# Fourteen input projections as three products of rounded parts, with GpSimd making the weights' low parts and the keys ahead of the low-rank products

## The chip, the cores and the metric

The kernel runs on one core of one Trainium2 chip. The metric is the device time of one execution in microseconds (us). The core has five engines, each with its own queue of instructions in program order: TensorE (matrix products into PSUM), VectorE, ScalarE, GpSimd and SyncE (which only issues transfers). They wait for each other by semaphores.

## What is computed

One layer of a streaming encoder for 512 tokens of width 1024, in float32. The tokens are normalized and modulated to h; h is multiplied by one combined input matrix whose columns feed three groups of heads; their outputs go through an output projection; a top-4-of-32 mixture of experts follows.

```python
cond = silu(c); mod = cond @ ada_w + ada_b          # 6 x 1024: sh1, sc1, g1, sh2, sc2, g2
h  = rms_norm(x, norm1) * (1 + sc1) + sh1
zp = h @ w_in                                       # columns: RWKV 1024, pool 256, q 512, k 512, v 512, f 8
# RWKV group: z = z + (previous token's z - z) * mu, then r, k, v and the inputs of three low-rank products
w_log = -softplus(-(w0 + tanh(wd) @ w_up)) - 0.5;  a = sigmoid(a0 + ad @ a_up);  g = sigmoid(gd) @ g_up
kk = k * k_k; kk = kk / norm(kk); k = k * (1 + (a - 1) * k_a)      # then a recurrence over the tokens
# pool group: trailing means of z over 2, 4, 8, 16 tokens, minus z, a small matrix per group
# fox group: softmax(q k^T / 8 + D[t] - D[s]) v with D = cumsum(log_sigmoid(f + b))
x = x + g1 * (concat(y_rwkv, y_pool, y_fox) @ w_out)
h = rms_norm(x, norm2) * (1 + sc2) + sh2;  x = x + g2 * moe(h);  out = rms_norm(x, norm_f)
```

## The kernel before

The input projections are worked feature by feature. hT holds h transposed as eight blocks of 128 features by 512 tokens. A **set** is one block of 128 output columns: eight products (k = 0..7) of a 128x128 block of weights with hT[k] (128x512), added up in one PSUM bank. There are 23 sets: eight "rw" (the RWKV columns), four "q", four "k", two "pz" (pool), one "f" of 8 columns, and four "v", where tokens and features change places. A float32 product appears in the trace as two matmul records, so a set has 16. The experts' weights, in contrast, are split already: ScalarE rounds them to float32r (w_hi, L1490), VectorE subtracts (w_lo, L1496), and TensorE makes three products of rounded parts for each (L2147).

The order of the work is written out once, in `plan()`, and every engine walks the same list `STEPS` and does its own part of each step. A **job** is a step with a PSUM bank; three banks are used in turn, so TensorE starts job n only when job n-3 has been read (`read_by`). Who reads a job stands in `READERS`: ScalarE copies rw, q, k, v and pz; VectorE reads "ada" and "rk"; "f" is read first by VectorE (L1033), then by ScalarE.

In a step "rw", ScalarE copies the bank to one of two buffers, and VectorE shifts it by one token and mixes (L968, L969, semaphore `shifted`); ScalarE's copy of rw n waits for the shift of rw n-2. Behind each rw, q and k step stands a step "acc": VectorE adds one of sixteen 1 MB pieces of `ada_w`, scaled by a value of cond, to a running sum of 128x2048 (L957, or L959 for the first of eight). The sum of eight pieces is then multiplied by a row of ones in four "ada" jobs (L1220), behind the first q set for the first half, between the value sets for the second.

SyncE's queue (`late_load`) brings these pieces into three buffers: piece i waits for sum i-2. The input weights arrive in six blocks of 512 columns in two buffers, block n waiting for the last job of block n-2. All are in one queue in order: blocks rw 0-3 and rw 4-7, pieces 0 to 4, two loads of `ada_b`, the q block, pieces 5 to 8, the k block, pieces 9 to 12, the pool and f block, pieces 13 to 15, the v block.

Before the list, ScalarE and VectorE each scale four blocks of hT (L723, L889), and VectorE builds masks and other constants (L893 to L920). GpSimd builds masks at the start, then waits for rw 7, fills 128x1024 with zeros and writes them to 17 blocks of `y_rows` (8.7 MB, L636), then makes the window sums of the pool columns (L643 to L648) and small products in the solve stage (L658 to L665).

"lora" are six low-rank products, "kkn" two sums for the norm of kk. At step kkn VectorE runs a chain (L980 to L1002); at pz 0 ScalarE takes exponentials (L767 to L771) and VectorE makes elementwise products (L1007 to L1019) that the solve stage needs. At step f VectorE reads the bank, waits for ScalarE's logarithm, scans (L1062) and finishes the pool windows (L1077 to L1082); only behind that does it read the "ada" jobs between the values. The fox attention, the solve stage, the recurrence, the output projection and the experts follow.

Of the kernel before, what the change touches and what calls it, by code (L numbers as in the profile page):

```python
# [15 lines left out]
F32 = mybir.dt.float32  # L16
# [62 lines left out]
def plan():  # L79

    def acc(i):
        return [("acc", i)]

    def turned(first):
        return [("ada", b) for b in range(first, first + 4)]

    steps = []
    for n in range(8):
        steps += [("rw", n)] + acc(n)
    steps += [("q", 0)] + turned(ADA_FIRST)  # L90
    for n in range(4):
        steps += ([("q", n)] if n else []) + acc(8 + n)
    steps += [("lora", n) for n in range(6)]
    steps += [("kkn", ct) for ct in range(CT)]
    for n in range(4):
        steps += [("k", n)] + acc(12 + n)
    steps += [("rk", ct) for ct in range(CT)]
    steps += [("pz", 0), ("pz", 1), ("f", 0)]
    for t in range(TT):
        steps += [("v", t), ("ada", ADA_FIRST + 4 + t)]  # L100
    pairs = FH * TT // 2
    early = 2
    steps += [("fox", u) for u in range(early)]
    steps += [("trAV", t) for t in range(TT)] + [("pm", 0)] + [("trBK", t) for t in range(TT)] + [("pm", 1)]
    solve = []
    for q in range(2):
        for kind in ("MP", "M"):
            solve += [(kind, q, par) for par in range(2)]
    fill = [[("NP", 0, 0), ("NP", 0, 1)], [("NP", 1, 0), ("NP", 1, 1)], [("NV", 0), ("NV", 1)]]
    for lv in range(1, LEVELS):  # L110
        solve += [("T", q, lv) for q in range(2)]
        if lv <= len(fill):
            solve += fill[lv - 1]
        for q in range(2):
            if lv < LEVELS - 1:
                solve.append(("XA", q, lv))
            solve.append(("XB", q, lv))
    solve += [("W", t) for t in range(TT)]
    for kind in ("QY", "GH"):
        solve += [(kind, q, cc) for q in range(2) for cc in range(2)]  # L120


    done = early
    for n, s in enumerate(solve):
        steps.append(s)
        while (done - early) * len(solve) < (n + 1) * (pairs + 2 - early):
            steps.append(("fox", done))
            done += 1
    while done < pairs + 2:
        steps.append(("fox", done))  # L130
        done += 1
    return steps
# [3 lines left out]
JOBS = [s for s in STEPS if s[0] not in ("fox", "acc")]  # L136
JOB = {s: n for n, s in enumerate(JOBS)}


# [5 lines left out]
def build(nc, a, out):  # L145
    with ExitStack() as ctx:
# [78 lines left out]
        R0 = early.enter_context(nc.sbuf_tensor("R0", [P, LATE], F32))  # L225
        Wt = early.enter_context(nc.sbuf_tensor("Wt", [P, 24576], F32))
        W3 = lambda off, x, y: Wt[:, off:off + x * y].rearrange("p (x y) -> p x y", x=x)
        R3 = lambda off, x, y: Rc(off, off + x * y).rearrange("p (x y) -> p x y", x=x)

        blk = [W3(4096 * s, KT, 512) for s in range(2)]  # L230

        def pair(off):
# [111 lines left out]
        h_act = sem("h_act")  # L344
        h_dve = sem("h_dve")
        bias2_in = sem("bias2_in")
        late_in = [sem(f"late_in{s}") for s in range(3)]
# [4 lines left out]
        cst_pool = sem("cst_pool")  # L352
        cst_dve = sem("cst_dve")
        cond_sig = sem("cond_sig")
# [75 lines left out]
        bias_lo = sem("bias_lo")  # L430
        bias_raw = sem("bias_raw")
        gm_rdy = sem("gm_rdy")
# [73 lines left out]
        def _(sp):  # L506
# [36 lines left out]
            def w_out_part(lo, hi, landed):  # L543
                sp.dma_start(w_out_sb[:, lo:hi, :], w_out_v[:, lo:hi, :]).then_inc(landed, 16)

            w_out_part(5, KT, wout_in)
            sp.dma_start(x_sb, a["x"][0].rearrange("(t p) d -> p t d", p=P)).then_inc(x_in, 16)
# [16 lines left out]
        def blk_ready(eng, b):  # L564
            n = BLK_OF[b]
            count = 16 * (n // 2 + 1)
            pf = BLK_OF[("pf", 0)]
            if n % 2 == pf % 2 and n >= pf:
                count += 16
            eng.wait_ge(blk_in[n % 2], count)  # L570


        @block.gpsimd
        def _(pool):
# [57 lines left out]

            job_done(pool, ("rw", 7))
            zero_src = Wt[:, 11264:11264 + D]
            link(g.memset(zero_src, 0.0))
# [37 lines left out]
        def _(act):  # L673
# [48 lines left out]
            for k in range(1, KT, 2):  # L722
                s.activation(hT[:, k, :], hT[:, k, :], ACT.Identity, scale=modc[:, KT + k:KT + k + 1],  # L723
                             bias=modc[:, k:k + 1]).then_inc(h_act, 1)

            for step in STEPS:
                kind = step[0]
# [29 lines left out]
                if kind == "rw" and step[1] >= 2:  # L757
                    act.wait_ge(shifted, step[1] - 1)
                if kind == "q" and step[1] == 2:
                    for ct in range(CT):  # L760
                        act.wait_ge(kk_raw, ct + 1)
                        s.activation(Kh[:, ct, :], Bh[:, ct, :], ACT.Square).then_inc(kk_sq, 1)
                if kind == "pz" and step[1] == 0:
                    for ct in range(CT):
# [52 lines left out]
                elif kind == "W":  # L817
                    ins = s.activation(W12[step[1]], b.rearrange("p (h w k) -> p h w k", h=RH, w=2), ACT.Copy)
                elif kind == "QY":
                    q, cc = step[1], step[2]  # L820
                    ins = s.activation(of_chunks(Yin, q, cc), b.rearrange("p (c j w s) -> p c j w s", c=CT, j=2, w=2)[:, :, :, 1, :],
                                       ACT.Copy)
                elif kind == "GH":
                    q, cc = step[1], step[2]
                    act.wait_ge(y_zero, 16)
                    ins = s.activation(GH[:, :, 4 * q + cc:4 * q + cc + 3:2, :],
                                       b.rearrange("p (j x m) -> p x j m", j=2, x=CT), ACT.Copy)
                ins.then_inc(act_read, 1)
                if kind == "f":
                    act.wait_ge(act_read, reads_through("A", step))  # L830
# [16 lines left out]
        def _(dve):  # L847
# [40 lines left out]
            for k in range(0, KT, 2):  # L888
                v.tensor_scalar(hT[:, k, :], hT[:, k, :], modc[:, KT + k:KT + k + 1], modc[:, k:k + 1],  # L889
                                ALU.mult, ALU.add).then_inc(h_dve, 1)  # L890

            dve.wait_ge(cst_pool, 1)
# [26 lines left out]
            link(v.reciprocal(rcnt[:], rcnt[:]))  # L919
            v.memset(stmp[:], 0.0).then_inc(cst_dve, 1)  # L920

# [3 lines left out]
            for step in STEPS:  # L925
# [66 lines left out]
                if kind == "kkn":  # L992
# [11 lines left out]
                                    ALU.subtract).then_inc(logs, 1)  # L1004
                if kind == "pz" and step[1] == 0:
                    for ct in range(CT):
# [114 lines left out]
        def _(pe):  # L1121
# [44 lines left out]
            for step in STEPS:  # L1166
# [54 lines left out]
                elif kind in ("rw", "q", "k", "pz", "f"):  # L1221
# [9 lines left out]
                    w = blk[BLK_OF[key] % 2]  # L1231
                    for k in range(KT):
                        if step == ("rw", 0):
# [497 lines left out]
        def _(dve):  # L1731
# [23 lines left out]
            dve.wait_ge(cst_pool, 2)  # L1755
            v.tensor_scalar(braw[:], braw[:], low_row[:, 0:1], None, ALU.mult).then_inc(bias_raw, 1)
            dve.wait_ge(bias_raw, 1)
            v.scalar_tensor_tensor(out=bparts[:], in0=bparts[:].bitcast(F32), scalar=low_row[:, 1:2], in1=braw[:],
# [544 lines left out]
```

## Time and profile before

| | us |
|---|---|
| median of 3 runs | 1601.86 (1599.86 to 1604.1) |
| profiled execution | 1599.61 |
| its span | 1597.9 |
| TensorE busy | 1528.8 (96%) |
| VectorE busy | 1349.7 (84%) |
| ScalarE busy | 989.9 (62%) |
| GpSimd busy | 187.1 (12%) |

The profile's page gives busy time of each engine and 40 equal slices of the span. The trace behind it is asked for the chain of waits, for stretches of time, for single engines. Busy time of TensorE is modelled for overlapping matmuls, so the pace of a group of matmuls is better read from the chain, where 16 or 48 stand in one piece. The input projections lie between 38 and 212 us of the span.

### The profile page before, as it was taken

Reading aid. Unit: us, or ns where it says so; the run is one execution under the profiler, and the core shown is the slowest. Engines: PE = TensorE matmul, PEld = TensorE weight load, DVE = VectorE, ACT = ScalarE, POOL = GpSimd, SP = SyncE. Lnnn points to the kernel's source line nnn. Section 1 sums busy time; section 2 is a strip of 40 time slices with the busy share of each in tenths; the row PEclk is TensorE's granted clock in tenths of the full one; section 3 lists DMA queues with packets and bytes.
Section 4 is the critical chain, followed back from the end, with each engine's and each line's share of the span. In section 5 each row is a group of like instructions: output and inputs, shape, how many; then the busy total and the mean of one; then the engine's idle time right before and its main releaser. Section 6 shows DMA issues by size and latency. Waiting matters only on the chain.

```text
span 1597.9 us, 22235 instructions
## 1 busy us (share of the span) xinstructions
PE 1528.8 (96%) x8326; PEld 1163.0 (73%) x8326; DVE 1349.7 (84%) x1053; ACT 989.9 (62%) x799; POOL 187.1 (12%) x223
## 2 busy tenths in 40 slices
PE   3999989998899999999999999999999999999996
PEld 2444357847578778888888888888888888888873
DVE  5557547477879999999999999999999999999987
ACT  4022233442467777777777777777777777777772
POOL 3000112000111100000010000001100000110061
PEclk9999999998999999999999999999999999999998
DMA  9686120124679998999999999999999999999992
GB/s 374 248 342 242 53 93 29 46 80 163 232 301 379 396 385 341 386 383 391 388 380 381 397 381 398 388 385 388 381 396 390 389 395 376 389 382 386 376 375 111
DMA packets 85926, 507.14 MB, mean 317 GB/s; under 512 B 11104, under 2 KB 12432, under 8 KB 33520
## 3 DMA queue, kind: packets, MB, share of 16 engines
q1 hardware_dynamic: 71040, 454.11, 72.4%
q0 software_dynamic: 9104, 34.08, 6.0%
q10 hardware_dynamic: 5728, 18.18, 2.9%
q8 instruction: 39, 0.64, 0.2%
q14 instruction: 15, 0.12, 0.0%
HBM read 477.51 MB, written 28.84 MB: 317 GB/s over the span
## 4 chain that ended last, share of the span: by engine, by line
PE 89%; DVE 6%; DMA 2%; issue 1%; ACT 1%; SPq 0%; POOL 0%; DVEq 0%; POOLq 0%; ACTq 0%
PE ps L2147 65%; PE ps L1235 8%; PE ps L2163 2%; PE ps L1241 2%; PE ps L1312 2%; DMA Wt<-in_ada_w 2%; PE ps L2126 2%; PE ps L2204 1%; PE ps L2136 1%; PE ps L2058 1%; PE ps L1210 1%; DVE w_lo L1496 1%; DMA h_rows<-R 1%; PE ps L1183 0%; DVE R L936 0%
## 5 line engine op out<-in xcount | busy, mean ns | idle before, releaser
L1496 DVE TENSOR_TENSOR w_lo<-w_raw,w_hi 128x2048 fp32r<-128x2048 f32 x384 | 866.0, 2289 | 73.6 <-ACT w_hi L1490 73.0
L1490 ACT ACTIVATE w_hi<-w_raw 128x2048 fp32r<-128x2048 f32 x384 | 736.2, 1919 | 279.9 <-PE ps L2147 279.9
L2147 PE MATMUL ps<-w_hi,xTh 128*128 128x512 f32 x1024 | 407.4, 398 | 5.4 <-DVE w_lo L1496 3.5
L2147 PE MATMUL ps<-w_lo,xTh 128*128 128x512 f32 x1024 | 401.6, 392 | 0.0
L2147 PE MATMUL ps<-w_hi,xTl 128*128 128x512 f32 x1024 | 275.7, 391 | 0.0
L2147 PEld LDWEIGHTS ps<-w_hi,xTh 128*128 128x128 f32 x1024 | 193.7, 189 | 52.6 <-issue 8.1
L2147 PEld LDWEIGHTS ps<-w_hi,xTl 128*128 128x128 f32 x1024 | 193.7, 189 | 40.9
L2147 PEld LDWEIGHTS ps<-w_lo,xTh 128*128 128x128 f32 x1024 | 193.7, 189 | 38.5
L2147 PE MATMUL ps<-w_hi,aTh 128*128 128x512 f32 x512 | 202.4, 395 | 0.0
L2147 PE MATMUL ps<-w_lo,aTh 128*128 128x512 f32 x512 | 199.4, 389 | 0.0
L2147 PE MATMUL ps<-w_hi,aTl 128*128 128x512 f32 x512 | 157.6, 389 | 0.0
L1538 POOL TENSOR_TENSOR carried<-iotaE 128x1 f32<-128x1 f32 x64 | 29.6, 462 | 997.1 <-PE ps L2126 900.7
L1235 PE MATMUL ps<-R,Wt 128*128 128x512 f32 (+1 forms) x304 | 131.3, 592 | 1.1 <-DVE R L889 1.1
L2147 PEld LDWEIGHTS ps<-w_hi,aTl 128*128 128x128 f32 x512 | 96.1, 188 | 20.1
L1235 PEld LDWEIGHTS ps<-R,Wt 128*128 128x128 f32 (+1 forms) x304 | 56.0, 185 | 75.1 <-issue 74.9
L2147 PEld LDWEIGHTS ps<-w_lo,aTh 128*128 128x128 f32 x512 | 96.2, 188 | 19.1 <-issue 0.2
L2147 PEld LDWEIGHTS ps<-w_hi,aTh 128*128 128x128 f32 x512 | 96.2, 188 | 19.1 <-issue 0.2
L1550 POOL DMA_INDIRECT xg<-h_rows,icol x30 | 86.4, 2882 | 4.4 <-issue 0.4
L736 ACT ACTIVATE R<-ps,fmx 128x128 f32<-128x128 f32 (+3 forms) x32 | 16.6, 523 | 44.6 <-DVE fmx L943 44.6
L1900 DVE SCALAR_TENSOR_TENSOR R<-R,sat 128x1024 f32<-128x1024 f32 x32 | 41.1, 1284 | 3.4
L1897 DVE TENSOR_SCALAR R<-ps 128x1024 f32<-128x1024 f32 x32 | 39.0, 1218 | 4.4 <-PE ps L2147 4.4
L1908 DVE TENSOR_TENSOR aTl<-ps,aTh 128x1024 fp32r<-128x1024 f32 x32 | 39.0, 1218 | 1.4 <-ACT aTh L1633 1.4
(409 smaller groups left out, 1379.9 us busy)
## 6 DMA issues: line engine op xcount, KB each, us to landing
w_raw<-in_moe_w_gu SPq DMA_DIRECT2D x256, 1024.0 KB, 6.6
w_raw<-in_moe_w_down SPq DMA_DIRECT2D x128, 1024.0 KB, 7.3
Wt<-in_ada_w SPq DMA_DIRECT2D x19, 1024.0 KB, 10.8
y_rows<-R ACTq DMA_DIRECT2D x30, 512.0 KB, 7.5
Wt<-in_w_in SPq DMA_DIRECT2D x5, 2048.0 KB, 13.7
y_rows<-Wt POOLq DMA_DIRECT2D x1, 8704.0 KB, 40.9
R<-in_ada_w SPq DMA_DIRECT2D x5, 1024.0 KB, 7.9
R<-in_x SPq DMA_DIRECT2D x2, 2048.0 KB, 10.3
```

The lines of the kernel that those rows point to most:

```text
L1235: ins = mm(b[0:rows, :], w[:, k, c:c + rows], hT[:, k, :], start=(k == 0), stop=(k == KT - 1))
L1241: ins = mm(b, hT[:, k, P * t:P * t + P], w[:, k, :], start=(k == 0), stop=(k == KT - 1))
L1312: ins = mm(b[r, CHUNK * i:CHUNK * i + CHUNK], lhs, rhs, start=True, stop=True)
L1490: nc.scalar.activation(w_hi[:, at[-1] % HI_SLOTS, :], w_raw[:, at[-1] % RAW_SLOTS, :], ACT.Copy).then_inc(hi_rdy, 1)
L1496: nc.vector.tensor_tensor(w_lo[:, s, :], w_raw[:, s, :], w_hi[:, at[-1] % HI_SLOTS, :].bitcast(F32), ALU.subtract).then_inc(lo_rdy, 1)
L1550: nc.gpsimd.indirect_dma_start(out=xg[s], out_offset=None, in_=h2_d, in_offset=bass.IndirectOffsetOnAxis(ap=ids, axis=0)).then_inc(xg_in[s ...
L1897: v.tensor_scalar(two(act_b), ps[:, 2:4, :], 1.0 - LIMIT, 1.0 + LIMIT, ALU.max, ALU.min).then_inc(up_rdy, 1)
L1900: v.scalar_tensor_tensor(out=act_b, in0=sig_b, scalar=sat[:, 0:1], in1=act_b, op0=ALU.min, op1=ALU.mult).then_inc(half_rdy, 1)
L1908: v.tensor_tensor(lo_part[:], ps[:, 4:6, :].rearrange("p b (k t) -> p (b k) t", k=4), hi_part[:].bitcast(F32), ALU.subtract).then_inc(lo_s ...
L2126: ins = nc.tensor.transpose(ps[:, 4 + k // 4, P * (k % 4):P * (k % 4) + P], xg[s][:, P * k:P * k + P], ident[:])
L2147: ins = mm(ps[:, bank0 + c, :], x[:, k, :], w[:, 512 * (banks * i + c):512 * (banks * i + c) + 512], start=(first and i == 0 and x is xh a ...
L2163: ins = nc.tensor.transpose(ps[:, 4 + k // 4, P * (k % 4):P * (k % 4) + P], act_b[:, 2 * P * j + i:2 * P * (j + 1):2], ident[:])
```

## The change

Fourteen sets (`SETS`: rw 2 to 7, q 0 to 3, k 0 to 3) become three groups of eight products of float32r operands: high part of the weights with high part of hT, high with low, low with high. ScalarE makes the eight high parts of hT and, two sets ahead, the high part of a set's weights (128x1024). VectorE makes the eight low parts of hT before its constants. GpSimd makes the low part of a set's weights in place. The four key sets move ahead of lora and kkn; rk moves behind pz; the elementwise work moves from pz 0 to f. GpSimd's zeros move behind lora 5 to another place in SBUF, and the wait for them moves from ScalarE's step GH to SyncE's load of `w_out`.

```diff
@@ plan @@
+    for n in range(4):
+        steps += [("k", n)] + acc(12 + n)
     steps += [("lora", n) for n in range(6)]
     steps += [("kkn", ct) for ct in range(CT)]
-    for n in range(4):
-        steps += [("k", n)] + acc(12 + n)
+    steps += [("pz", 0), ("pz", 1)]
     steps += [("rk", ct) for ct in range(CT)]
-    steps += [("pz", 0), ("pz", 1), ("f", 0)]
+    steps += [("f", 0)]
...
+SETS = [s for s in JOBS if s[0] in ("rw", "q", "k")][2:]
@@ SBUF: Wr is float32r in the place of Wt @@
+        blk_lo = [Wr3(4096 * s, KT, 512) for s in range(2)]
+        set_hi = [Wr3(16384 + 1024 * s, KT, P) for s in range(2)]
+        h_hi = Wr3(8192, KT, S)
+        h_lo = [Wr[:, 18432 + 512 * k:18944 + 512 * k] if k < 6 else Wr[:, 19456 + 512 * k:19968 + 512 * k]
+                for k in range(KT)]
@@ SyncE @@
+            sp.wait_ge(y_zero, 16)
             w_out_part(5, KT, wout_in)
...
+        def set_block(job):
+            kind, m = job
+            key = ("w_in", {"rw": 512 * (m // 4), "q": COL_Q, "k": COL_K}[kind])
+            return key, BLK_OF[key] % 2, slice(P * (m % 4), P * (m % 4) + P)
@@ GpSimd @@
-            job_done(pool, ("rw", 7))
-            zero_src = Wt[:, 11264:11264 + D]
+            for i, job in enumerate(SETS):
+                key, at, c = set_block(job)
+                pool.wait_ge(set_top, i + 1)
+                g.tensor_tensor(blk_lo[at][:, :, c], blk[at][:, :, c], set_hi[i % 2].bitcast(F32), ALU.subtract
+                                ).then_inc(set_rest, 1)
+
+            job_done(pool, ("lora", 5))
+            zero_src = Wt[:, 23552:23552 + D]
@@ ScalarE @@
+            def set_split(i):
+                key, at, c = set_block(SETS[i])
+                blk_ready(act, key)
+                if i >= 2:
+                    job_done(act, SETS[i - 2])
+                s.activation(set_hi[i % 2], blk[at][:, :, c], ACT.Copy).then_inc(set_top, 1)
+
+            for k in range(KT):
+                act.wait_ge(h_act if k % 2 else h_dve, k // 2 + 1)
+                s.activation(h_hi[:, k, :], hT[:, k, :], ACT.Copy).then_inc(h_act, 1)
+            for i in range(2):
+                set_split(i)
...
-                if kind == "q" and step[1] == 2:
+                if kind == "lora" and step[1] == 0:
+                    job_done(act, ("k", 3))
                     for ct in range(CT):
                         act.wait_ge(kk_raw, ct + 1)
                         s.activation(Kh[:, ct, :], Bh[:, ct, :], ACT.Square).then_inc(kk_sq, 1)
-                if kind == "pz" and step[1] == 0:
+                if kind == "f":                     # the exponentials
...
-                    act.wait_ge(y_zero, 16)         # in step GH
...
                 ins.then_inc(act_read, 1)
+                if step in SETS and SETS.index(step) + 2 < len(SETS):
+                    set_split(SETS.index(step) + 2)
@@ VectorE @@
+            for k in range(KT):
+                dve.wait_ge(h_act, KT // 2 + k + 1)
+                v.tensor_tensor(h_lo[k], hT[:, k, :], h_hi[:, k, :].bitcast(F32), ALU.subtract).then_inc(h_dve, 1)
...
-                if kind == "pz" and step[1] == 0:
+                if kind == "f":                     # the elementwise products
@@ TensorE @@
-                    for k in range(KT):
+                    if step in SETS:
+                        i = SETS.index(step)
+                        w_hi_, w_lo_ = set_hi[i % 2], blk_lo[BLK_OF[key] % 2][:, :, c:c + P]
+                        pe.wait_ge(h_act, KT // 2 + KT)
+                        pe.wait_ge(set_top, i + 1)
+                        for k in range(KT):
+                            mm(b, w_hi_[:, k, :], h_hi[:, k, :], start=(k == 0), stop=False)
+                        pe.wait_ge(h_dve, KT // 2 + KT)
+                        for k in range(KT):
+                            mm(b, w_hi_[:, k, :], h_lo[k], start=False, stop=False)
+                        pe.wait_ge(set_rest, i + 1)
+                        for k in range(KT):
+                            ins = mm(b, w_lo_[:, k, :], h_hi[:, k, :], start=False, stop=(k == KT - 1))
+                    for k in range(KT if step not in SETS else 0):
@@ VectorE, the experts' bias parts @@
-            v.tensor_scalar(braw[:], braw[:], low_row[:, 0:1], None, ALU.mult).then_inc(bias_raw, 1)
-            dve.wait_ge(bias_raw, 1)
+            link(v.tensor_scalar(braw[:], braw[:], low_row[:, 0:1], None, ALU.mult))
```

## Rows read from the trace of the kernel before

**Rows 1.** Chain of waits, 38 to 212 us: start, duration in us, engine, line.
```profile
38.55 62.04 PE ps L1235 x144
...
104.02 20.60 PE ps L1235 x48
124.62 1.05 PE ps L1247 x2
...
158.67 1.72 PE ps L1257 x4
...
181.08 7.06 PE ps L1241 x16
...
211.32 0.87 PE ps L1220 x2
```

**Rows 2.** Chain of waits in the experts' stage.
```profile
475.81 10.89 PE ps L2147 x48
```

**Rows 3.** Timeline of VectorE, 39 to 83 us: start, us, engine, line, operation, count, idle before.
```profile
39.68 0.42 DVE L893 CAST cumr<-zeroE 128x512 fp32r<-128x512 f32 x1
...
47.24 0.63 DVE L968 TENSOR_TENSOR R<-R 128x512 f32<-128x512 f32 x1
...
48.57 1.28 DVE L959 TENSOR_SCALAR Wt<-Wt,cs 128x2048 f32<-128x2048 f32 x1
...
67.05 0.69 DVE L968 TENSOR_TENSOR R<-R 128x512 f32<-128x512 f32 x1 [3.12 <-ACT R L778]
...
82.52 2.35 DVE L957 SCALAR_TENSOR_TENSOR R<-R,cs,Wt 128x2048 f32<-128x2048 f32 x1 [0.26 <-DMA R<-in_ada_w]
```

**Rows 4.** Timeline of ScalarE before the first set.
```profile
37.85 2.94 ACT L723 ACTIVATE R<-R,modc 128x512 f32<-128x512 f32 x4 [10.02 <-DVE modc L884]
```

**Rows 5.** Timelines of GpSimd (POOL) and VectorE where both are at work.
```profile
15.56 2.14 POOL L627 TENSOR_SCALAR_AFFINE_SELECT low_row<-low_row 128x1 f32<-128x1 f32 x1
...
15.30 2.35 DVE L865 SCALAR_TENSOR_TENSOR Wt<-Wt,cs 128x2048 f32<-128x2048 f32 x1 [1.83 <-DMA Wt<-in_ada_w]
...
167.98 1.21 POOL L643 TENSOR_TENSOR Wt<-R 128x527 f32<-128x527 f32 x1 [71.42 <-ACT R L797]
...
168.18 1.55 DVE L1014 TENSOR_TENSOR Wt<-R,Wt 128x512 f32<-128x512 f32 x1
...
174.83 1.06 POOL L643 TENSOR_TENSOR Wt<-R 128x527 f32<-128x527 f32 x1 [4.18 <-ACT R L797]
...
242.67 2.49 POOL L665 TENSOR_TENSOR Wt<-Wt,lvl 128x512 f32<-128x512 f32 x2
```

**Rows 6.** Timeline of SyncE's queue, 63 to 67 us.
```profile
63.95 0.33 SPq L520 DMA_DIRECT2D Wt<-in_ada_w  x1
...
66.28 0.38 SPq L527 DMA_DIRECT2D Wt<-in_w_in  x1
```

**Rows 7.** DMA issues, 66.0 to 66.7 us: KB each, median us to landing.
```profile
Wt<-in_w_in SPq DMA_DIRECT2D x1, 2048.0 KB, 13.7
```

**Rows 8.** Windows: length, busy time by engine, TensorE's granted clock, DMA share, GB/s.
```profile
28.00:30.00 2.00, 0.00 (x0) 0.00 (x0) 1.86 (x2) 0.00 (x0) 0.00 (x0) 1.00 0.97 393
32.00:34.00 2.00, 2.00 (x12) 1.40 (x10) 1.68 (x4) 0.00 (x0) 0.00 (x0) 0.50 1.04 386
```

**Rows 9.** Timeline of VectorE, 127 to 194 us.
```profile
127.94 0.49 DVE L980 TENSOR_SCALAR Wt<-R,cols 128x512 f32<-128x512 f32 x1 [5.79 <-ACT R L793]
...
147.02 2.35 DVE L957 SCALAR_TENSOR_TENSOR Wt<-Wt,cs,R 128x2048 f32<-128x2048 f32 x1
...
161.03 1.28 DVE L1007 TENSOR_TENSOR R<-Wt,R 128x512 f32<-128x512 f32 x2
...
171.84 0.68 DVE L1019 TENSOR_TENSOR Wt<-R,Wt 128x512 f32<-128x512 f32 x1
...
181.12 0.74 DVE L1033 TENSOR_SCALAR R<-ps,cols 8x512 f32<-8x512 f32 x1 [8.59 <-PE ps L1235]
...
193.90 0.69 DVE L1028 TENSOR_TENSOR R<-ps,R 128x512 f32<-128x512 f32 x1
```

More of the change, by code:

```diff
@@ L225, in build @@
         R0 = early.enter_context(nc.sbuf_tensor("R0", [P, LATE], F32))
-        Wt = early.enter_context(nc.sbuf_tensor("Wt", [P, 24576], F32))
+        wt_stack = ExitStack()
+        Wt = wt_stack.enter_context(nc.sbuf_tensor("Wt", [P, 24576], F32))
+        wt_stack.close()
+        Wr = early.enter_context(nc.sbuf_tensor("Wr", [P, 24576], F32R))
         W3 = lambda off, x, y: Wt[:, off:off + x * y].rearrange("p (x y) -> p x y", x=x)
@@ L230, in build @@
         blk = [W3(4096 * s, KT, 512) for s in range(2)]
+        Wr3 = lambda off, x, y: Wr[:, off:off + x * y].rearrange("p (x y) -> p x y", x=x)
+        blk_lo = [Wr3(4096 * s, KT, 512) for s in range(2)]
[3 more added lines that the diff above has]
+                for k in range(KT)]
         def pair(off):
@@ L345, in build @@
         h_dve = sem("h_dve")
+        set_top = sem("set_top")
+        set_rest = sem("set_rest")
         bias2_in = sem("bias2_in")
@@ L352, in build @@
         cst_pool = sem("cst_pool")
-        cst_dve = sem("cst_dve")
         cond_sig = sem("cond_sig")
@@ L430, in build @@
         bias_lo = sem("bias_lo")
-        bias_raw = sem("bias_raw")
         gm_rdy = sem("gm_rdy")
@@ L919, in _ @@
             link(v.reciprocal(rcnt[:], rcnt[:]))
-            v.memset(stmp[:], 0.0).then_inc(cst_dve, 1)
+            v.memset(stmp[:], 0.0)
             z_dest = [rT[:, 0, :], rT[:, 1, :], kT[:, 0, :], kT[:, 1, :], vT[:, 0, :], vT[:, 1, :],
```

## The prediction

> **What bounds the kernel now.** I read the chain of waits first. From 38.55 us to 212.19 us it is TensorE alone: nine sets of projections, four small products, three sets, the low-rank products, four sets of keys, and so on to the last set of values [rows 1]. Three sets of 16 matmul records take 20.60 us, so one set of float32 costs 6.87 us. The reader should see that in this stretch there is no waiting piece at all: whatever shortens a set shortens the run, until another engine becomes late. After 212 us the chain runs through the fox and solve stages and then through the experts; none of these is edited apart from two waits, so I price the change by when the last "ada" product of the values ends: 212.19 us before.
>
> **What a set gains.** The new set is 24 products of rounded operands of the same shape, 128x128 by 128x512. The experts' stage has exactly those: 48 in 10.89 us [rows 2], 0.227 us each, with a weight load for each as here. So a set becomes 24 x 0.227 = 5.45 us, 1.42 us less, and fourteen sets give 19.9 us. The bounds: this pace if nothing disturbs it, and no gain if it ran at float32's. I take the first, being the same instruction form.
>
> **What is late next: VectorE.** Before, VectorE built its constants (from 39.68 us) and was done at 47.24, then subtracted and scaled the first set's rows (1.33 us to 48.57), then made the first weighted sum (1.28) [rows 3]. Now eight low parts of hT come first. ScalarE finishes its four rows of hT at 40.79 (four in 2.94, so at most 0.73 us for 512 elements) [rows 4], then makes eight high parts of the same size, and VectorE's eight subtractions (0.69 each, as for any 128x512 of two inputs [rows 3]) end near 47.2. The constants then end near 54.7.
>
> GpSimd works at the same time now, once per set, on 128x1024 elements of two SBUF inputs. Two things must be bounded: how long it takes and what it does to VectorE. Duration: a flat sum of 527 elements takes 1.06 us undisturbed, that is 2.06 us for 1024; two sums of 512 in short runs take 2.49, that is 2.49 for 1024 [rows 5]. The new operands are in runs of 128, so I take 2.1. Effect: while GpSimd summed from 167.98 to 169.19, a VectorE sum that started at 168.18 took 1.55 us where this shape takes 0.69; it ended 0.54 us after GpSimd did. The other way round, a one-column select on GpSimd took 2.14 us and ended at 17.70, just after the 2048-element multiply-add of VectorE that began at 15.30 and ended at 17.65 [rows 5]. So the two exclude each other for whole instructions, and that multiply-add is the very form of the weighted sums ("acc"). One GpSimd difference costs VectorE between nothing (if it falls into idle time) and 2.5 us; inside a busy stretch I take 2.1.
>
> The Trainium skill (GPSIMD Engine Reference, section 1, Specifications) says the same more broadly: GpSimd's SBUF interfaces are shared with VectorE, against instructions with two SBUF inputs and those in a two-port mode. The trace agrees for both kinds of rows above; by that rule the constants' copies are held up too. Section 3.1 of that page gives 4497 ns for 2048 elements, an estimate of 2.25 us here, by which the sum below would be about 1 us higher; section 4.1 advises VectorE for elementwise work.
>
> **The sum, in order of time.** Two sets stay float32: TensorE is at 38.55 + 13.74 = 52.3. The first two GpSimd differences fall into the constants: 54.7 + 2 x 2.1 = 58.9. First shift and first sum: 61.5. From there each set asks VectorE for 1.33 + 2.35 us and GpSimd for 2.1 of the shared access, 5.8 us where TensorE asks 5.45. So the third sum ends at 61.5 + 11.6 = 73.1; before, it had ended by 63.95, when SyncE's next transfer, which waits for it, went out [rows 6]. SyncE's queue is in order: behind that transfer stand the two bias loads, then the query weights. All move by 9.2 us, so the query weights, issued at 66.28 and landed 13.7 us later [rows 6, 7], land at 89.2, not 80.0. TensorE finishes the eighth set at 52.3 + 6 x 5.45 = 85.0, and ScalarE cannot copy the first query set before the block is there: 89.2 + 1.2 + 0.2 = 90.6. A stall of **5.6 us**. Before, the set began at 93.5, 13 us after landing.
>
> The sixth sum's operand follows the query weights in the queue; VectorE waited for it until 82.52 [rows 3], 2.5 us behind them: now 91.7. Behind it stand three sums and two shifts, 3 x 2.35 + 2 x 1.33 = 9.7, and two to three GpSimd differences, 5.3: 106.7. The four "ada" products need that eighth sum. TensorE ended the first query set at 90.6 + 5.45 = 96.1: a stall of **10.6 us**. The four take 4 x 0.87 = 3.5 [last of rows 1]: 110.2.
>
> A second cost of standing still: TensorE has nothing to do from 28 to 30 us, and from 32 to 34 its granted clock is 0.50, which is 1.2 GHz [rows 8]: 1.0 us of work lost in that window alone. For the two longer stalls I take 1.5 each (between 0 and 3): 113.2. Seven more sets at 5.45 end at 151.4. The weights of the keys need not be waited for: SyncE issues them near 87 and what follows has 20 us or more.
>
> The low-rank products and norms began at 124.62, and four sets of keys behind them ended at 158.67 [rows 1], so they took 34.05 - 27.48 = 6.6 us; they now wait 0.4 for two squares that ScalarE makes first: 158.4. Before, the same work was done at 158.67 [rows 1]. So up to here everything gained is gone, -0.3.
>
> **The tail.** VectorE's work on keys and decays ran from 127.94 to 147.02, 19.1 us [rows 9], hidden under four sets of keys. Now the keys are ahead. It starts when the low-rank results are out, 4.0 us after the last key (before 3.3, plus the squares), at 155.4, and ends at 174.5 without GpSimd; the zero fill and six window sums of 1.06 share the access, of which I count 4.5 (0 to 7.4): 179.0. Then the elementwise products, 161.03 to 172.5 before with the last of them started at 171.84 [rows 9], with 0.9 of waiting and 1.7 of GpSimd in it: 8.9, and 1.4 for the "rk" products: 189.3. Only then comes VectorE's reading of "f". TensorE ends "f" at 158.4 + 2 x 6.87 + 1.72 + 6.87 = 180.7. Before, VectorE read it at once (181.12), and 13.5 us later (193.90 + 0.69) had read the first "ada" sum behind it [rows 9], which frees the PSUM bank of the third value set. Now that is 202.8, where TensorE wants the bank at 180.7 + 2 x 7.74 = 196.2: a stall of **6.6 us**, and about 1 of slow clock behind it. The end: 202.8 + 15.5 + 1 = 219.3, against 212.19: **+7.1 us**.
>
> The zero fill of 8.7 MB moves from 95 to about 158 us; its only waiters are now behind 210 us, so it costs nothing, and the loads that it slowed run free, none of them late. The ordinary wait that replaces a semaphore in the bias parts is priced at nothing: same instruction, same order.
>
> The profiled execution took 1599.61 us (span 1597.9), the median of the runs is 1601.86. +7.1 makes 1606.7 of the profiled one and 1609.0 of the median; I forecast **1609**. About 0.3%, 4.8 us, is what a measurement can tell from no change.
>
> **Rivals.**
> 1. *GpSimd hides in VectorE's pauses.* VectorE stands idle about 3 us per set, 3.12 before one shift [rows 3]. If the differences fall there, or the exclusion is much shorter than a whole instruction: constants end at 54.7, the third sum at 54.7 + 1.33 + 1.28 + 2 x 3.68 = 64.7, the query weights land at 80.7 in time, the eighth sum ends at 83.2 + 9.7 = 92.9 against 90.5 (stall 2.4), the tail is 2.0 late: -19.9 + 2.4 + 0.4 + 2.0 = -15.1, **1587**. It decides when the third sum ends before about 68. For it: the idle time. Against it: [rows 5], and a sum needs 2.35 us in one piece. Chance 0.27.
> 2. *Half of it:* each difference costs VectorE about 1 us. The third sum ends near 68, both stalls shrink by 6 to 7 us together: **1601**, no change to be seen. Chance 0.20.
> 3. *Slower GpSimd:* 2.5 us per difference. Eight of them stand ahead of the "ada" products, +0.4 each, and two in the tail, and clocks lost in full: +12, **1614**. Chance 0.08.
> 4. The forecast, 0.45; a tenth of it reaches under 0.3%.
>
> Slower: 0.41 + 0.08 = 0.49. Same: 0.20 + 0.03. Faster: 0.28, the first rival and the fast end of the second. Likeliest case alone: 1605 to 1615. With the others: 1586 to 1616.
>
> **What would show it.** After: rounded products 0.227 us apart, sets of 5.45 us; GpSimd differences of 2.1 us or more, sums on VectorE well over 2.35 us where they meet; SyncE's query weights issued near 75; TensorE idle 5 to 6 us before the first query set and 10 before the first "ada" product; then 6 before the third value set. It is wrong if the sums keep 2.35 us, or if the query weights go out before 68 us.

## The result, and the profile after

The changed kernel takes 1606.23 us (median of 7, 1603.76 to 1608.84), the kernel before in the same comparison 1601.41 (7 runs). The ratio is 1.0033, 95% interval 1.0023 to 1.0044: slower by about 5 us, where 1609 against 1601.86 was forecast. The profiled execution took 1605.35 us, its span 1603.6, 5.7 more than before.

The page of the kernel after: busy time by engine, and the shares of the chain.

```profile
PE 1515.3 (94%) x8438; PEld 1185.5 (74%) x8438; DVE 1375.7 (86%) x1061; ACT 1006.8 (63%) x821; POOL 231.8 (14%) x237
...
PE 81%; DVE 12%; DMA 2%; ACT 2%; issue 1%; SPq 0%; POOL 0%; DVEq 0%; ACTq 0%; POOLq 0%
```

TensorE is busy 13.5 us less and the kernel takes longer, so the difference is waiting. The chain of waits of the kernel after, 38 to 218 us (start, us, engine, line), shows who is waited for:

```profile
41.70 4.91 DVE Wr L932 x8
46.98 2.33 DVE R L937
49.34 2.27 DVE R L939
...
66.59 2.77 DVE R L1010
...
78.28 13.21 DMA R<-in_ada_w
91.51 3.17 DVE R L999
...
104.07 2.27 DVE Wt L999
106.48 5.69 PE ps L1262 x8
112.17 1.86 PE ps L1280 x8
114.03 1.82 PE ps L1283 x8
115.85 1.81 PE ps L1286 x8
...
199.64 8.64 PE ps L1296 x16
...
216.00 0.87 PE ps L1262 x2
```

Where [rows 1] had TensorE alone, VectorE and one transfer now hold most of the chain from 41.70 to 106.48. After that the query and key sets run as three groups of eight in 1.81 us each (up to 1.86 in the first set behind a pause): 5.44 a set, 0.227 a product. TensorE's waits of the kernel after in the same stretch (us in total, times, longest):

```profile
PE ps L1262 <- DVE Wt L999: 9.0, 1, 9.0
PE ps L1280 <- ACT Wr L755: 4.7, 1, 4.7
PE ps L1296 <- DVE R L1070: 4.0, 1, 4.0
```

They stand ahead of the first four "ada" products, of query set 0 and of the third value set. The next two timelines show VectorE and GpSimd of the kernel after at the third shift (66.59). A shift took 0.69 us in [rows 3]. First VectorE's timeline, then GpSimd's:

```profile
58.15 0.63 DVE L1010 TENSOR_TENSOR R<-R 128x512 f32<-128x512 f32 x1
...
64.21 2.34 DVE L999 SCALAR_TENSOR_TENSOR Wt<-Wt,cs 128x2048 f32<-128x2048 f32 x1
66.59 2.76 DVE L1010 TENSOR_TENSOR R<-R 128x512 f32<-128x512 f32 x1
69.39 0.75 DVE L1011 SCALAR_TENSOR_TENSOR R<-R,cols 128x512 f32<-128x512 f32 x1
70.06 2.35 DVE L999 SCALAR_TENSOR_TENSOR R<-R,cs,Wt 128x2048 f32<-128x2048 f32 x1
```
```profile
46.34 5.17 POOL L654 TENSOR_TENSOR Wr<-Wt,Wr 128x1024 fp32r<-128x1024 f32 x2 [28.19 <-ACT Wr L755]
61.22 2.52 POOL L654 TENSOR_TENSOR Wr<-Wt,Wr 128x1024 fp32r<-128x1024 f32 x1 [9.72 <-ACT Wr L755]
65.95 2.86 POOL L654 TENSOR_TENSOR Wr<-Wt,Wr 128x1024 fp32r<-128x1024 f32 x1 [2.21 <-ACT Wr L755]
```

GpSimd's difference of 65.95 is issued inside VectorE's sum, which ends at 66.55, and ends at 68.81, 2.26 later. The shift that follows the sum takes 2.76 us, 2.07 more than undisturbed, and ends at 69.35. So VectorE stands still for the rest of the GpSimd instruction, nearly the whole of it. The sums keep their 2.34 to 2.35 us here: it is the shift behind the sum that is held up. The SyncE queue shows what hangs on it; it answers to [rows 6]:

```profile
73.75 0.65 SPq L538 DMA_DIRECT2D Wt<-in_w_in  x1
```

The query weights go out 7.5 us later than before and take 15.2 us, so they land at 88.95. ScalarE waits for them until 89.02, TensorE for ScalarE's copy until 90.22. Timeline of TensorE, kernel after, at the first two waits:

```profile
90.22 3.58 PE L1280 MATMUL ps<-Wr 128*128 128x512 f32 x8 [4.66 <-ACT Wr L755]
93.64 2.01 PE L1283 MATMUL ps<-Wr 128*128 128x512 f32 x8
95.50 1.97 PE L1286 MATMUL ps<-Wr 128*128 128x512 f32 x8
106.48 5.69 PE L1262 MATMUL ps<-Wt,R 128*128 128x512 f32 x8 [9.01 <-DVE Wt L999]
```

After each wait the first products are slow: query set 0 takes from 90.22 to 97.4, 1.8 us more than 5.44; the four "ada" products 5.69 where they took 3.4 before. The windows of the kernel after (columns as in [rows 8]) show the granted clock:

```profile
88.00:90.00 2.00, 0.00 (x0) 0.00 (x0) 0.00 (x0) 0.98 (x2) 0.00 (x0) 1.00 1.02 424
90.00:92.00 2.00, 1.78 (x4) 1.49 (x5) 0.49 (x1) 1.51 (x3) 1.85 (x1) 0.52 1.02 426
...
102.00:104.00 2.00, 0.00 (x0) 0.00 (x0) 1.97 (x3) 0.29 (x1) 0.73 (x1) 0.50 0.81 336
...
108.00:110.00 2.00, 2.00 (x3) 0.67 (x2) 0.69 (x1) 0.00 (x0) 0.00 (x0) 0.50 1.09 404
...
112.00:114.00 2.00, 2.00 (x10) 1.64 (x9) 1.83 (x3) 0.00 (x0) 0.00 (x0) 1.00 0.21 86
```

At the first wait (85.56 to 90.22) the clock is still at 2.4 GHz up to 90 us and is at 1.2 GHz in the first us of the work behind it. At the second (97.47 to 106.48) it is at 1.2 GHz before the wait ends and in the first us of the work, and at 2.4 GHz again from 112 us on.

**The account.** I measure each kernel by one stretch: from the first set of projections to the end of the last "ada" product. Before it is 38.55 to 212.19 [rows 1], 173.6 us; after it is 38.91 (TensorE's timeline) to 216.87, 178.0: **+4.3 us**. The terms: fourteen sets, 14 x (6.87 - 5.44) = 20.0 gained; 4.7 + 1.8 lost at query set 0; 9.0 + 2.3 at the "ada" products; 4.0 + 1.8 at the third value set (8.64 instead of 6.87); 0.4 among the low-rank products. The sum is +4.0: 24.0 lost against 20.0 gained. What lies behind the stretch took 1385.7 us in the profile before, 1386.7 after and up to 1391.9 in the experiments (experiment 4), and the start differs by 1.7 us (38.17 to 39.84), so the stretch is the better scale for one profile.

### The profile page after: what moved, and what is told of

Read it like the earlier page. It is cut to its first block, busy times and chain, and to the rows that moved or that the text cites. A ratio compares the mean times of both kernels' runs of the same rounds, so it can differ in the third digit from the quotient of the medians.

```text
span 1603.6 us, 22526 instructions
## 1 busy us (share of the span) xinstructions
PE 1515.3 (94%) x8438; PEld 1185.5 (74%) x8438; DVE 1375.7 (86%) x1061; ACT 1006.8 (63%) x821; POOL 231.8 (14%) x237
## 4 chain that ended last, share of the span: by engine, by line
PE 81%; DVE 12%; DMA 2%; ACT 2%; issue 1%; SPq 0%; POOL 0%; DVEq 0%; ACTq 0%; POOLq 0%
PE ps L2201 65%; PE ps L2217 2%; PE ps L1367 2%; DMA Wt<-in_ada_w 2%; PE ps L2180 2%; PE ps L1296 1%; PE ps L2258 1%; DVE w_lo L1551 1%; DMA R<-in_ada_w 1%; PE ps L1280 1%; PE ps L1286 1%; PE ps L1283 1%; PE ps L2190 1%; PE ps L2112 1%; PE ps L1252 1%
## 5 line engine op out<-in xcount | busy, mean ns | idle before, releaser
L654 POOL TENSOR_TENSOR Wr<-Wt,Wr 128x1024 fp32r<-128x1024 f32 x14 | 43.5, 3116 | 83.1 <-ACT Wr L755 83.1
L1957 DVE SCALAR_TENSOR_TENSOR R<-ps,R 128x1024 f32<-128x1024 f32 x32 | 39.2, 1224 | 1.1
## 6 DMA issues: line engine op xcount, KB each, us to landing
Wt<-in_w_in SPq DMA_DIRECT2D x5, 2048.0 KB, 15.2
R<-in_x SPq DMA_DIRECT2D x2, 2048.0 KB, 10.6
```

The source lines that it names most:

```text
L654: g.tensor_tensor(blk_lo[at][:, :, c], blk[at][:, :, c], set_hi[i % 2].bitcast(F32), ALU.subtract).then_inc(set_rest, 1)
L1957: v.scalar_tensor_tensor(out=two(act_b), in0=ps[:, 0:2, :], scalar=LIMIT, in1=two(act_b), op0=ALU.min, op1=ALU.mult).then_inc(act_rdy, 1)
```

## The experiments

Ratios are against runs of the kernel before in the same comparison (medians 1601.74 us for experiments 1 to 4, 1601.48 for 5 to 8, 1602.20 for 9), the stretch against 173.6. Those medians and the 1601.41 beside the changed kernel agree within 0.8 us, so medians of different comparisons are set side by side below to about 1 us.

| | median us, runs | ratio, 95% interval | stretch us |
|---|---|---|---|
| after | 1606.23, 7 | 1.0033, 1.0023 to 1.0044 | 178.0 (+4.3) |
| e1_no_shared_access | 1593.96, 5 | 0.9951, 0.9938 to 0.9964 | 166.7 (-7.0) |
| e2_order_only | 1610.29, 6 | 1.0048, 1.0034 to 1.0062 | 180.3 (+6.7) |
| e3_gpsimd_only | 1601.17, 12 | 0.9998, 0.9989 to 1.0007 | 173.7 (0.0) |
| e4_low_on_vector | 1599.23, 12 | 0.9980, 0.9970 to 0.9990 | 171.5 (-2.2) |
| e5_bias_early | 1602.30, 11 | 1.0007, 0.9998 to 1.0015 | 174.2 (+0.6) |
| e6_pool_behind_ada | 1600.93, 11 | 0.9992, 0.9983 to 1.0001 | 172.0 (-1.6) |
| e7_vector_bias_pool | 1588.73, 6 | 0.9915, 0.9899 to 0.9931 | 160.9 (-12.7) |
| e8_ada_behind_q1 | 1585.48, 4 | 0.9897, 0.9881 to 0.9912 | 155.8 (-17.9) |
| e9_ada_behind_q1_gpsimd | 1590.80, 5 | 0.9931, 0.9917 to 0.9945 | 162.6 (-11.1) |

The theory (A): GpSimd's differences block VectorE for whole instructions, VectorE is then late, and so are SyncE's transfers behind it. Its rivals: (B) the new order of steps alone costs the time; (C) the loss is the new load on ScalarE and VectorE, GpSimd's share of the access mattering little.

**1. No GpSimd difference.** The low parts of the weights are left out; GpSimd only passes the signal on, and the third group multiplies the high part again.

```diff
-                g.tensor_tensor(blk_lo[at][:, :, c], blk[at][:, :, c], set_hi[i % 2].bitcast(F32), ALU.subtract
-                                ).then_inc(set_rest, 1)
+                g.memset(carried[:, 0:1], 0.0).then_inc(set_rest, 1)
+                pool.wait_ge(set_rest, i + 1)
-                            ins = mm(b, w_lo_[:, k, :], h_hi[:, k, :], ...)
+                            ins = mm(b, w_hi_[:, k, :], h_hi[:, k, :], ...)
```

> The changed kernel, but GpSimd writes one column elsewhere instead of subtracting 128x1024, and the third group of products takes the high part of the weights a second time (so the low part of the weights is left out of the result; TensorE's work is the same). Theory A (VectorE and GpSimd exclude each other on SBUF, which makes the weighted sums late): VectorE's shift takes 0.69 us instead of 2.76, the third sum ends near 66 us instead of 72.4, no wait before the first query set, at most 3 us before the first ada product; about 14 us faster than the changed kernel, near 1592. Theory B (the eight low parts of hT ahead of the constants, and the order of the transfers, make the sums late; GpSimd only overlaps): the third sum still ends at 70 us or later and the time stays within 4 us of the changed kernel.

Measured: 12.3 us below the changed kernel. VectorE's timeline of this kernel around the third sum, and TensorE's waits:

```profile
59.77 0.69 DVE L1010 TENSOR_TENSOR R<-R 128x512 f32<-128x512 f32 x1
60.49 0.75 DVE L1011 SCALAR_TENSOR_TENSOR R<-R,cols 128x512 f32<-128x512 f32 x1
61.16 2.35 DVE L999 SCALAR_TENSOR_TENSOR R<-R,cs,Wt 128x2048 f32<-128x2048 f32 x1
```
```profile
PE ps L1296 <- DVE R L1070: 4.0, 1, 4.0
PE ps L1262 <- DVE Wt L999: 3.3, 1, 3.3
```

The same shift takes 0.69 instead of 2.76, the third sum ends 8.9 us earlier (63.5 for 72.4), and the wait ahead of query set 0 is gone. The 8.9 us add up: four meetings with a GpSimd difference are gone, and the profile starts 0.7 earlier. Two of the meetings were in the constants (the rows of 46.98 and 49.34 in the chain, 2.33 and 2.27 us, take 0.29 and 0.23 here), two between the first and the third sum. Everything else of the change is still there, so this is theory A, and C falls for most of the loss. The tail's 4.0 us stays: it has another cause.

**2. Only the new order,** in the kernel before: keys ahead of lora, rk behind pz, the elementwise work at f. No product is split.

```diff
+    for n in range(4):
+        steps += [("k", n)] + acc(12 + n)
     steps += [("lora", n) for n in range(6)]
     steps += [("kkn", ct) for ct in range(CT)]
...
+    steps += [("pz", 0), ("pz", 1)]
     steps += [("rk", ct) for ct in range(CT)]
+    steps += [("f", 0)]
```

> The kernel before with only the new order: keys ahead of lora and kkn, rk behind pz, exponentials and elementwise products at f; all sets float32, the zeros where they were. Theory A with its tail: VectorE's chain starts 4 us behind the last key, its reading of f comes 5 to 6 us after TensorE ends f, and the third value set waits 3 to 4 us and then runs at a low clock for some us: 4 to 6 us slower than before, near 1607. Rival (the order is free, the whole loss comes from the early waits): within 1 us of the kernel before.

Measured: 8.5 us slower than before, the stretch 6.7 longer. Timeline of TensorE in this kernel, third value set:

```profile
201.74 8.83 PE L1242 MATMUL ps<-Wt,R 128*128 128x512 f32 x16 [3.96 <-DVE R L1029]
```

The same wait of 4.0 and the same slow set behind it (2.0 more than 6.87) as in the changed kernel: the order costs this by itself, and gains nothing. The wait (4.0), the slow clock behind it (2.0) and the wait for the squares (0.4) make 6.4 of the 6.7 seen; I had expected 4 to 6.

**3. Only GpSimd's work,** in the kernel before: fourteen differences of 128x1024 of unused columns, one behind each of the first fourteen sets. Nobody waits for them.

```diff
+            for i, job in enumerate([s for s in JOBS if s[0] in ("rw", "q", "k")][:14]):
...
+                job_done(pool, job)
+                link(g.tensor_tensor(idle, idle, idle2, ALU.subtract))
```

> The kernel before, with fourteen GpSimd subtractions of 128x1024 beside it, one behind each of the rw, q and first two k sets, on idle SBUF, for which nobody waits. Theory A: VectorE's operations of two SBUF inputs stretch by about 2 us once a set, but VectorE stands idle 3.1 us a set, so TensorE still never waits and the time is within 1.5 us of the kernel before; the exclusion costs only where sets are shorter or VectorE is behind. Rival (the exclusion costs about 2 us wherever it occurs): 4 us slower or more.

Measured: no change (interval 0.9989 to 1.0007), and the stretch the same to 0.1 us. GpSimd's and VectorE's timelines of this kernel:

```profile
60.68 2.34 POOL L644 TENSOR_TENSOR Wt<-Wt 128x1024 f32<-128x1024 f32 x1 [4.53 <-PE ps L1243]
```
```profile
61.33 2.24 DVE L976 TENSOR_TENSOR R<-R 128x512 f32<-128x512 f32 x1 [1.58 <-ACT R L786]
```

The exclusion is there (2.24 for a shift of 0.69), yet costs nothing, because VectorE has some 3 us of idle time per set as long as a set takes 6.87. So the price of GpSimd's work is not in itself: it arises where a set has shrunk to 5.44. The difference takes 2.34 us with nothing in its way, not the 2.1 of the prediction.

**4. The low parts on VectorE,** GpSimd idle; the rest is the changed kernel.

```diff
+            def set_low(i):
+                dve.wait_ge(set_top, i + 1)
+                v.tensor_tensor(blk_lo[at][:, :, c], blk[at][:, :, c], set_hi[i % 2].bitcast(F32), ALU.subtract
+                                ).then_inc(set_rest, 1)
```

> The changed kernel with the low parts of the weights made on VectorE (0.69 us for 512 elements, so 1.2 for 1024) behind its shift, and GpSimd idle. Theory A: a set asks VectorE for 3.7 + 1.2 = 4.9 us instead of 3.7 + 2.1 = 5.8, less than TensorE's 5.45; the third sum ends near 69 us (72.4 in the changed kernel), the query weights go out 3 us earlier, the waits before the first query set and before ada together shrink by 6 to 8 us: near 1598. Rival (VectorE has too much to do and GpSimd relieves it): the sums end later than in the changed kernel and it is slower than 1606.

Measured: 7.0 us below the changed kernel; the profiled execution (1604.73) is the slowest of its twelve, so only its stretch, 6.5 shorter, is used. VectorE's timeline of this kernel:

```profile
64.80 1.22 DVE L931 TENSOR_TENSOR Wr<-Wt,Wr 128x1024 fp32r<-128x1024 f32 x1
```

VectorE makes the same difference in 1.22 us. Handed to GpSimd it costs VectorE 2.07: taking the work off VectorE took more of its time than doing it. The third sum ends at 68.3 (72.4). Not all is gained: query set 0's third group now waits 2.4 us, since its low part is made behind a sum that waits for its transfer, and the "ada" products still wait 4.6. The result is slightly below the kernel before (interval 0.9970 to 0.9990).

**5. The bias loads earlier.** SyncE issues the two `ada_b` loads ahead of piece 3 instead of between piece 4 and the query weights.

```diff
+                        if i == 3:
+                            sp.dma_start(Rc(2 * D, LATE), a["ada_b"][0, 2 * D:LATE]...).then_inc(bias2_in, 16)
+                            sp.dma_start(Rc(LATE, 6 * D), a["ada_b"][0, LATE:6 * D]...).then_inc(bias2_in, 16)
```

> The changed kernel with the two loads of ada_b (2 MB) ahead of piece 3 in SyncE's queue, where the DMA engines stand idle, instead of behind piece 4. Theory A with the queue: the query weights, still issued near 73 us, land near 82 instead of 89 and TensorE no longer waits for the first query set; piece 5 lands near 85 instead of 91.5 and the eighth sum ends near 100.5 instead of 106.4, still behind TensorE, so the first ada product comes 6 us sooner: near 1600. Rival (the landing is set by the issue, which waits for the third sum, and the bias loads cost nothing there): within 1.5 us of the changed kernel.

Measured: 3.9 us below the changed kernel (stretch 3.8), where 6 was expected. Waits of TensorE, then a row of VectorE's timeline, of this kernel:

```profile
PE ps L1263 <- DVE Wt L1000: 10.7, 1, 10.7
PE ps L1297 <- DVE R L1071: 4.0, 1, 4.0
```
```profile
86.82 3.73 DVE L1000 SCALAR_TENSOR_TENSOR R<-R,cs,Wt 128x2048 f32<-128x2048 f32 x1 [0.68 <-DMA R<-in_ada_w]
```

The wait ahead of query set 0 is gone. The query weights still go out at 73.32, behind the third sum, but the two bias loads no longer stand just ahead of them, and they land sooner (DMA issues of this kernel):

```profile
Wt<-in_w_in SPq DMA_DIRECT2D x1, 2048.0 KB, 11.0
```

That is 11.0 us for 15.2. The "ada" products, though, wait for the sums and not for this set, and now for 10.7 us instead of 9.0. Counted from the first set, the piece for the sixth sum lands 5.2 us earlier than in the changed kernel (86.82 - 39.42 for 91.51 - 38.91), the eighth sum ends 4.7 earlier, since GpSimd's difference holds up this sum longer (3.73 for 3.17), and the four products take 6.46 us for 5.69. That leaves 4.0.

**6. The pool windows later.** VectorE finishes them behind its reading of "ada" 5 of the values, not at f.

```diff
-                if kind == "f":
+                if step == ("ada", ADA_FIRST + 5):
```

> The changed kernel with VectorE's work on the pool windows (5.3 us) moved from f to behind its reading of the second ada job of the values. Theory A with its tail: VectorE reads the bank for the third value set near 194 instead of 199 us, TensorE wants it near 195, so the wait of 4.0 us and the slow clock behind it (1.8 us) go: near 1600.5. Rival (something else is due there just as late): at most 2 us faster.

Measured: 5.3 us below the changed kernel (stretch 5.9). The chain of this kernel:

```profile
187.05 7.13 PE ps L1296 x16
...
195.04 6.87 PE ps L1296 x16
```

The value set that took 8.64 behind a wait takes 6.87 without one; 4.0 + 1.8 is the whole difference. The two early waits stay (9.2 and 4.6).

**7. Experiments 4, 5 and 6 together.**

> Low parts of the weights on VectorE, ada_b loaded early, and the pool windows' work behind the second ada job of the values, all three. Theory A: the third sum ends near 68 us, the query weights land near 78, piece 5 near 81, the eighth sum ends near 93, TensorE waits at most 2 us before ada and not at all for the third value set: near 1586, 15 us faster than the kernel before. Rival (the waits give way to others of the same length): 1594 or more.

Measured: 12.8 us below the kernel before, 17.5 below the changed one. The three gains alone, 7.0 + 3.9 + 5.3, are 16.2: they add up and a little more, which I have not traced further. One wait of 3.2 us is left ahead of the "ada" products.

**8. The first "ada" products behind query set 1,** on top of 7.

```diff
-    steps += [("q", 0)] + turned(ADA_FIRST)
     for n in range(4):
-        steps += ([("q", n)] if n else []) + acc(8 + n)
+        steps += [("q", n)] + (turned(ADA_FIRST) if n == 1 else []) + acc(8 + n)
```

> The kernel of all three, with the four ada products behind the second query set instead of the first, which gives the eighth sum 5.45 us more. Theory A: no wait at ada, 1 to 3 us faster than the kernel of all three, near 1584. Rival: the pieces 10 and later, whose buffer the ada products hold, come late and the key sets or what follows them wait, so no gain.

Measured: 1585.48, the fastest, 16.0 us below the kernel before and 20.8 below the changed one. The stretch is 17.9 shorter than before, of the 20.0 that fourteen sets give.

**9. The same with the low parts on GpSimd again** (the edit of experiment 4 undone, those of 5, 6 and 8 kept).

> The fastest kernel so far (ada_b early, pool windows' work late, ada products behind the second query set), but with the low parts of the weights on GpSimd again as in the changed kernel. Theory A: the eighth sum ends near 102 us as in the run with ada_b early, TensorE ends the second query set near 96.5 and waits 5 to 6 us, with 2 us of slow clock behind it: 7 to 8 us slower than with VectorE, near 1593. Rival (once the order of the transfers and of the ada products is mended, it does not matter who subtracts): within 2 us of 1585.5.

Measured: 5.3 us above experiment 8 (stretch 6.8). The chain of this kernel:

```profile
101.52 6.15 PE ps L1262 x8
```

The wait ahead of the "ada" products is back, 5.4 us, and they take 6.15 instead of 3.4. So the engine for the low part matters in the mended order too, though less than I expected (7 to 8).

## Why the prediction was right

Direction and mechanism held. The stalls were taken too long and their slow clock too short; the largest miss is in the tail. The direction was not safe, though: it is the difference of 20.0 gained and 24.0 lost, and the prediction itself gave "slower" only 0.49. The measured 4.8 us is just the size that it named as the least that can be told from no change; the interval, 1.0023 to 1.0044, settles that it is a loss.

- **What a set gains**: 5.45 forecast, 5.44 measured, 20.0 us in all. Right.
- **The exclusion**: 2.1 us per meeting forecast, 2.07 measured on the shift of 66.59, so rival 2's 1 us is not what is seen. It holds for whole instructions and in both directions (3.83 us in the last section). One named sign was wrong in its place: the prediction wanted sums well over 2.35 us and called itself wrong if they kept 2.35. Ahead of the first "ada" products all but one do keep it, because GpSimd's difference is issued while a sum runs and then holds up the shift behind it, 2.76 for 0.69; only the sixth sum, at 91.51, is itself held up (3.17). The Trainium skill (GPSIMD Engine Reference, section 1, Specifications) names this contention, for instructions with two SBUF inputs and those in a two-port mode. The trace agrees for two inputs; it also shows a conversion with one input held up, at 49.34, 2.25 us beside GpSimd's pair and 0.23 before, of which no row says whether it ran in such a mode. Section 4.1's advice to do elementwise work on VectorE is borne out by experiments 4 and 9: 7.0 and 5.3 us.
- **VectorE's queue**: first shift at 58.9 forecast, 58.15 seen; a set 5.8, 5.85 (64.21 to 70.06); third sum 73.1, 72.4; query weights landing 89.2, 88.95; eighth sum 106.7, 106.34. The difference itself was taken too short (2.1 for 2.34), but some of them fell into idle time. The key weights went out at 100.93, not near 87, and were still in time: no wait stands ahead of the key sets.
- **The two early stalls**: 5.6 and 10.6 forecast, 4.7 and 9.0 seen, 2.5 us less. The slow clock behind them gave 1.1 back: 1.8 and 2.3 for 1.5 each. So the keys end at 150.3, 1.1 us ahead of the forecast 151.4.
- **The tail** is the mis-sized term: 6.6 + 1 forecast, 4.0 + 1.8 seen. VectorE's chain of keys and decays began at 153.80 (155.4 forecast) and took 22.5 us to 176.3 where I had 23.6; the elementwise work was 0.4 shorter; so the reading of f came at 186.1, not 189.3. For GpSimd's share of that chain I had counted 4.5 us; undisturbed it takes 19.1 [rows 9], so the share was 3.4. GpSimd's fill and window sums, from 155.70 to 177.47, are busy for 8.8 us, and part of that falls on VectorE's reciprocals, where it costs nothing. Two rows of the kernel after show one such pair, first VectorE's, then GpSimd's:

```profile
162.25 3.35 DVE L1038 RECIPROCAL Wt<-Wt 128x512 f32<-128x512 f32 x1
```
```profile
164.94 1.05 POOL L667 TENSOR_TENSOR Wt<-R 128x527 f32<-128x527 f32 x1 [6.48 <-ACT R L835]
```

  The reciprocal, with one input, and the window sum overlap, and both keep their own time.
- **Sum**: +7.1 forecast, +4.7 seen at the last "ada" product (216.87 for 212.19, of it 0.4 from a later start). The miss of 2.4 is the bank's reading, 199.6 for 202.8, less the 0.8 by which the slow clock there was under-sized.

Rival 1's condition, a third sum before 68 us, is met in experiment 1 (63.5). The time is then 1593.96 us, faster than before, though not the 1587 of the rival: that had 2.0 for the tail, where 4.0 + 2.0 was lost, and 2.4 at the "ada" products, where it was 3.3 + 3.0. And experiment 3 shows that GpSimd does hide in VectorE's pauses, in the kernel before. With the shorter sets the pauses are gone. Rival 3's slower GpSimd was half true (2.34 us), but not of the sum.

Not settled: how the remaining 0.3 us of the stretch and the about 1 us behind it arise. Runs of one kernel differ by more than that (1603.76 to 1608.84 for the kernel after).

## What to carry to other kernels

Shortening TensorE's work helps until the next engine's work per step fills the shorter step; add up that engine's time per step at the new pace, including what another engine on the shared access takes from it. A difference that VectorE makes in 1.22 us cost it 2.07 when GpSimd made it, and cost the kernel nothing while VectorE had 3 us a set to spare. Then look at what waits for the late engine in a queue that works in order: here two bias loads ahead of the weights, and a read of PSUM behind 5.3 us of work on the pool windows, cost 3.9 and 5.3 us and were mended by moving a few lines.

## What the runs showed of the hardware that was not expected

- **What a wait of 3 us or more cost besides its length hardly depended on the length.** The four first "ada" products take 3.4 us before. They took 6.46 behind a wait of 3.3 us (experiment 1), 6.60 behind 3.2 (7), 5.83 behind 4.6 (4), 6.15 behind 5.4 (9), 5.69 behind 9.0 (after), 5.52 behind 9.2 (6) and 6.46 behind 10.7 (5): 2.1 to 3.2 us more each time. A wait of 1.0 us ahead of the fourth of them (experiment 8) left no such mark: the clock stays at 2.4 GHz, that product takes 1.13 us on the timeline where one takes 1.02, and the next group 1.85. Windows of experiment 1, columns as in [rows 8]:

```profile
92.00:94.00 2.00, 0.48 (x1) 0.50 (x2) 1.97 (x3) 1.97 (x3) 0.06 (x1) 0.58 0.96 400
94.00:96.00 2.00, 2.00 (x3) 0.67 (x2) 0.69 (x2) 1.72 (x2) 0.00 (x0) 0.50 1.05 410
...
98.00:100.00 2.00, 2.00 (x5) 0.97 (x4) 0.69 (x1) 0.00 (x0) 0.00 (x0) 0.72 1.10 427
```

  The wait ends at 93.52. The clock falls to 1.2 GHz within the window of 92 to 94 us and comes back within that of 98 to 100, when the "ada" products are nearly done.

- **Both engines stretch.** In experiment 3 GpSimd's difference, 2.34 us alone, shows as 3.83 from 112.18: VectorE's sum of 111.45 ran until 113.80, and the difference took 2.21 us from there. A long GpSimd row can thus be a wait for VectorE.
